# Storing the residual early, adding the feed-forward's output onto it by accumulating DMAs from GpSimd, and taking the last two block products by token tile

## What is computed

```python
x = x + rms_norm(merged @ w_o, norm_mix_post)
hf = rms_norm(x, norm_ff_pre)
ff = jnp.square(jax.nn.relu(hf @ w_ff_in)) @ w_ff_out     # 1024 -> 4096 -> 1024
return x + rms_norm(ff, norm_ff_post)
```

## Time and profile before

| what | us |
|---|---|
| median of 3 runs (785.39 to 787.23) | 785.5 |
| the profiled execution, its own time | 785.12 |
| its span, first to last instruction | 783.4 |
| TensorE busy in it | 765.7 (98%) |
| VectorE busy | 529.3 (68%) |
| ScalarE busy | 365.2 (47%) |
| GpSimd busy | 58.4 (7%) |
| mean granted TensorE clock | 0.996 of full speed |

### The profile page before, as it was taken

The page is one execution under the profiler, slowest core; times in us unless marked ns, Lnnn a source line. Parts: engine busy times, 40 slices in busy tenths (PEclk is TensorE's granted clock), DMA queues, the critical chain, the costliest instruction groups (busy, mean ns, idle before and its releaser), DMA issues.

```text
span 783.4 us, 9921 instructions
## 1 busy us (share of the span) xinstructions
PE 765.7 (98%) x3640; PEld 640.7 (82%) x3640; DVE 529.3 (68%) x883; ACT 365.2 (47%) x609; POOL 58.4 (7%) x110
## 2 busy tenths in 40 slices
PE   7999999999999999999999999999999999999994
PEld 6888888888887888888888998888887888878873
DVE  5624667677777336885635779746895579667897
ACT  4522656666565744232325545544443444334542
POOL 3000000022223003000001200000000000000002
PEclk9999999999999999999999999999999999999998
DMA  8333232212132532326331452136003620262002
GB/s 295 109 114 101 70 92 79 83 55 82 55 83 80 188 101 61 114 75 242 107 108 54 161 186 57 54 139 211 27 3 104 259 65 1 56 240 81 0 1 108
DMA packets 91581, 80.29 MB, mean 102 GB/s; under 512 B 2833, under 2 KB 77585, under 8 KB 91537
## 3 DMA queue, kind: packets, MB, share of 16 engines
q1 hardware_dynamic: 90864, 79.70, 31.5%
q10 hardware_dynamic: 672, 0.01, 0.0%
HBM read 77.60 MB, written 2.10 MB: 102 GB/s over the span
## 4 chain that ended last, share of the span: by engine, by line
PE 90%; DVE 6%; ACT 1%; DMA 1%; issue 0%; SPq 0%; POOL 0%; DVEq 0%; POOLq 0%; ACTq 0%
PE acc L1382 26%; PE acc L1384 26%; PE acc L1383 26%; DVE w_lo L1213 2%; PE aux L1383 1%; PE aux L1384 1%; PE aux L1382 1%; DVE sum L1236 1%; DMA w_raw<-in_w_in 1%; PE aux L1569 1%; PE aux L1495 1%; PE aux L1494 1%; PE aux L1504 1%; PE acc L1523 1%; PE acc L1520 1%; PE aux L1477 1%
## 5 line engine op out<-in xcount | busy, mean ns | idle before, releaser
L1382 PE MATMUL acc<-actB_hi,w_hi 128*128 128x512 f32 (+1 forms) x544 | 207.3, 381 | 0.8 <-DVE sum L1318 0.8
L1384 PE MATMUL acc<-actB_hi,w_lo 128*128 128x512 f32 (+1 forms) x544 | 205.4, 378 | 0.0
L1383 PE MATMUL acc<-actB_lo,w_hi 128*128 128x512 f32 (+1 forms) x544 | 205.2, 377 | 0.0
L931 DVE TENSOR_TENSOR w_lo<-w_raw,w_hi 128x1024 fp32r<-128x1024 f32 x72 | 87.8, 1223 | 83.9 <-ACT w_hi L648 83.1
L1382 PEld LDWEIGHTS acc<-actB_hi,w_hi 128*128 128x128 f32 x544 | 102.5, 188 | 19.6 <-DVE w_lo L1209 1.6
L1384 PEld LDWEIGHTS acc<-actB_hi,w_lo 128*128 128x128 f32 x544 | 102.4, 188 | 18.9
L1383 PEld LDWEIGHTS acc<-actB_lo,w_hi 128*128 128x128 f32 x544 | 102.5, 188 | 18.1
L648 ACT ACTIVATE w_hi<-w_raw 128x1024 fp32r<-128x1024 f32 x72 | 75.4, 1052 | 71.1 <-PE acc L1384 68.8
L1382 PE MATMUL acc<-w_hi,actB_hi 128*128 128x512 f32 x160 | 62.7, 392 | 1.5 <-DVE actB_lo L941 1.3
L1384 PE MATMUL acc<-w_hi,op_lo 128*128 128x512 f32 x160 | 63.5, 397 | 0.0
L1383 PE MATMUL acc<-w_lo,op_hi 128*128 128x512 f32 x160 | 63.4, 396 | 0.0
(11 more groups left out here) (192 smaller groups left out, 1292.1 us busy)
## 6 DMA issues: line engine op xcount, KB each, us to landing
w_raw<-in_w_in SPq DMA_DIRECT2D x44, 512.0 KB, 3.9
w_raw<-in_w_ff_in SPq DMA_DIRECT2D x32, 512.0 KB, 4.0
down_raw<-in_w_ff_out SPq DMA_DIRECT2D x16, 1024.0 KB, 6.9
w_raw<-in_w_b SPq DMA_DIRECT2D x8, 512.0 KB, 3.6
w_raw<-in_w_a SPq DMA_DIRECT2D x8, 512.0 KB, 3.5
w_raw<-in_w_o SPq DMA_DIRECT2D x8, 512.0 KB, 3.8
x<-in_x SPq DMA_DIRECT2D x4, 512.0 KB, 7.5
x<-in_x SPq DMA_DIRECT2D x1, 2048.0 KB, 9.0
```

What stands on the lines that cost most here:

```text
L931: nc.vector.tensor_tensor(w_lo[:, j], w_raw[:, j], w_hi[:, j].bitcast(F32), ALU.subtract).then_inc(lo_made, 1)
L1382: nc.tensor.matmul(o, a_hi, b_hi, start=first, stop=False)
L1383: nc.tensor.matmul(o, a_hi, b_lo, start=False, stop=False)
L1384: return nc.tensor.matmul(o, a_lo, b_hi, start=False, stop=last)
```

## The change

Four things.

1. SyncE stores the four tiles of `x1` to the result in chunk 0 of the feed-forward, behind the loads of that chunk and ahead of the load of `g_ff_post`. They count on a new semaphore, `x1_stored`.
2. The final sums of VectorE go. `scale` multiplies a half in place by `rstd` and the gain in one `scalar_tensor_tensor` (`sum * rstd * g`), and GpSimd issues, for each of the eight halves, a DMA with `accum_op=ALU.add` that adds the 128 x 512 tile onto the result in HBM. GpSimd waits for `x1_stored` before the first and for all eight at the end. The gains into `down_raw` go too. The SBUF reserved for DMAs issued by GpSimd is doubled (`SCRATCH`).
3. TensorE takes the last two products by token tile: P3 and P2 for p = 0, then P3 and P2 for p = 1.
4. VectorE, ScalarE and GpSimd follow that order: the merges for p = 0, then for p = 1, with the scaling of tiles 2 and 3 between them; the adds of tile 2 are written before the `rstd` of tile 0 on GpSimd, those of tile 3 before the `rstd` of tile 1, the other four last.

```diff
-SCRATCH = 1024
+SCRATCH = 2048
...
+LAST_TWO = [(CHUNKS - 1, "P3"), (CHUNKS - 1, "P2")]
...
@@ SyncE @@
                 load_down(c, 3)
                 if c == 0:
+                    for t in range(TT):
+                        sp.wait_ge(x1_made, t + 1)
+                        sp.dma_start(out_v[:, t], x1[:, t]).then_inc(x1_stored, 16)
                     sp.wait_ge(pe_done, UNIT_DONE[U_FF - 1])
                     sp.dma_start(g_ff_post[:], norm_ff_post[0:1, :].to_broadcast([P, D])).then_inc(g_ff_in, 16)
-            for n, t in enumerate((2, 3)):
-                sp.wait_ge(y_made, n + 1)
-                sp.dma_start(out_v[:, t], x1[:, t]).then_inc(stored, 16)
-            for n, (t, h) in enumerate(((0, 1), (0, 0), (1, 1), (1, 0))):
-                cols = slice(h * COL, (h + 1) * COL)
-                sp.wait_ge(y_made, 2 + n + 1)
-                sp.dma_start(out_v[:, t, cols], x1[:, t, cols]).then_inc(stored, 16)
-            sp.wait_ge(stored, 16 * 6)
@@ GpSimd @@
-            for first, n in ((2, 0), (0, 4)):
...
+            def add_out(n, src, t, half):
+
+                pool.wait_ge(y_made, n + 1)
+                nc.gpsimd.dma_start(out_v[:, t, half * COL:(half + 1) * COL], src,
+                                    accum_op=ALU.add).then_inc(stored, 16)
+
+            ff_half(slice(2, 4), 2)
+            ff_rstd(2, 3)
+            ff_rstd(3, 4)
+            pool.wait_ge(x1_stored, 16 * TT)
+            add_out(0, sum6[:, 0], 2, 1)
+            add_out(1, sum4[:, 0], 2, 0)
+            ff_half(slice(0, 1), 5)
+            ff_rstd(0, 6)
+            add_out(2, sum6[:, 1], 3, 1)
+            add_out(3, sum4[:, 1], 3, 0)
+            ff_half(slice(1, 2), 7)
+            ff_rstd(1, 8)
+            for p in range(2):
+                add_out(4 + 2 * p, sum1[:, p], p, 1)
+                add_out(5 + 2 * p, sum2[:, p], p, 0)
+            pool.wait_ge(stored, 16 * 2 * TT)
@@ ScalarE @@
             for p in range(2):
-                ff_square(4 + p, sum1[:, p], 1, p)
-            for p in range(2):
-                ff_square(6 + p, sum2[:, p], 0, p)
+                ff_square(4 + 2 * p, sum1[:, p], 1, p)
+                ff_square(5 + 2 * p, sum2[:, p], 0, p)
@@ VectorE @@
+                def scale(o, half, t):
+
+                    dve.wait_ge(rstd_ff, {2: 1, 3: 2, 0: 3, 1: 4}[t])
+                    nc.vector.scalar_tensor_tensor(o, o, rstd[:, 4, t:t + 1],
+                                                   g_ff_post[:, half * COL:(half + 1) * COL],
+                                                   ALU.mult, ALU.mult).then_inc(y_made, 1)
...
+            dve.wait_ge(g_ff_in, 16)
             for p in range(2):
...
+                bank_done("P3", p)
+                merge(sum1[:, p], aux[:, 2 + p], sum1[:, p], signal=ff_ready)
+                if p:
+                    scale(sum1[:, 0], 1, 0)
+                    scale(sum2[:, 0], 0, 0)
+                else:
+                    scale(sum6[:, 0], 1, 2)
+                    scale(sum4[:, 0], 0, 2)
+                bank_done("P2", p)
+                merge(sum2[:, p], acc[:, p], sum2[:, p], signal=ff_ready)
+                if p == 0:
+                    scale(sum6[:, 1], 1, 3)
+                    scale(sum4[:, 1], 0, 3)
+            scale(sum1[:, 1], 1, 1)
+            scale(sum2[:, 1], 0, 1)
@@ TensorE @@
+            for p in range(2):
+                for c, name in LAST_TWO:
+                    bank_free(c, name, p)
+                    for h in range(2):
+                        if p == 0:
+                            operands(c, name, h)
+                        m = item_product(c, name, h, p)
+                    m.then_inc(pe_done, 1)
```

More of the change, by code:

```diff
@@ L164, in _pe_counts @@
             u = U_FF + product_item(c, name, 0)
-            if (c, name) != (CHUNKS - 1, PRODUCTS[-1]):
-                n += 1
-                unit_done[u] = n
+            if (c, name) in LAST_TWO:
+                continue
+            n += 1
+            unit_done[u] = n
             for p in range(2):
@@ L171, in _pe_counts @@
             unit_done[u + 1] = n
+    for p in range(2):
+        for c, name in LAST_TWO:
+            n += 1
+            bank_done[U_FF + product_item(c, name, 1), p] = n
     return unit_done, bank_done
@@ L628, in _, with ff_rstd, ff_half @@
                     inv_sqrt(ssq[:, 3, t:t + 1], 3, t, rstd_x1)
-            for first, n in ((2, 0), (0, 4)):
-                pair = slice(first, first + 2)
-                pool.wait_ge(ff_squared, n + 2)
-                after(nc.gpsimd.tensor_scalar(ssq_eps[:, 1, pair], ssq[:, 5, pair], EPS, None, ALU.add))
-                for p in range(2):
[L634 to L638, removed]
+            def ff_rstd(t, squared):
+                pool.wait_ge(ff_squared, squared)
+                after(nc.gpsimd.tensor_tensor(var_eps[:, 4, t:t + 1], ssq_eps[:, 1, t:t + 1],
+                                              ssq[:, 4, t:t + 1], ALU.add))
+                power(4, t, rstd_ff)
+            def ff_half(tiles, squared):
+                pool.wait_ge(ff_squared, squared)
+                after(nc.gpsimd.tensor_scalar(ssq_eps[:, 1, tiles], ssq[:, 5, tiles], EPS, None, ALU.add))
+            def add_out(n, src, t, half):
[18 more added lines that the diff above has]
+            pool.wait_ge(stored, 16 * 2 * TT)
         @block.scalar
@@ L1344, in _ @@
                             ins.then_inc(ff_ready, 1)
[L1345 to L1348, removed]
                     lo_ahead(item(c, at + 1))
[L1350 to L1355, removed]
-                            gain(2 + p, sum4[:, p], 0, 2 + p)
@@ L1357, in _ @@
-                    if last and name == "P3":
-                        for p in range(2):
-                            gain(4 + p, sum1[:, p], 1, p)
-                        for t in (2, 3):
-                            dve.wait_ge(rstd_ff, t - 1)
-                            dve.wait_ge(gained, 4)
-                            nc.vector.scalar_tensor_tensor(x1[:, t], down_raw[:, t, 0], rstd[:, 4, t:t + 1], x1[:, t],
-                                                           ALU.mult, ALU.add).then_inc(y_made, 1)
@@ L1365, in _ @@
-            for p in range(2):
-                dve.wait_ge(pe_done, BANK_DONE[UNITS - 1, p])
-                nc.vector.tensor_tensor(sum2[:, p], acc[:, p], sum2[:, p], ALU.add).then_inc(ff_ready, 1)
-                gain(6 + p, sum2[:, p], 0, p)
-                dve.wait_ge(rstd_ff, 3 + p)
-                for h in (1, 0):
-                    cols = slice(h * COL, (h + 1) * COL)
-                    dve.wait_ge(gained, 5 + p if h else 7 + p)
-                    nc.vector.scalar_tensor_tensor(x1[:, p, cols], down_raw[:, p, 0, cols], rstd[:, 4, p:p + 1],
-                                                   x1[:, p, cols], ALU.mult, ALU.add).then_inc(y_made, 1)
+            dve.wait_ge(g_ff_in, 16)
@@ L1660, in _ @@
                 for name in PRODUCTS:
-                    if (c, name) == (CHUNKS - 1, PRODUCTS[-1]):
-                        for p in range(2):
-                            bank_free(c, name, p)
-                            for h in range(2):
-                                if p == 0:
-                                    operands(c, name, h)
-                                m = item_product(c, name, h, p)
-                            m.then_inc(pe_done, 1)
+                    if (c, name) in LAST_TWO:
                         continue
```

9 lines of the change are left out of this document (2 added, 7 removed).

## The result

The changed kernel takes 790.0 us (median of 7 runs, 789.53 to 791.88) against 785.5 us: ratio 1.006, 95% interval 1.0051 to 1.0069. It is slower by 4.5 us, and outside the predicted range. The profiled execution took 790.44 us, its span is 788.7.

What follows compares the result with a forecast made beforehand. The prediction took the 10.0 us tail behind TensorE's last matmul as the bound, 3.8 us of it order. Span end 775.8 + 3.0 + 1.0 + 2.9 + 0.4 = 783.1 against 783.4; forecast 785.2 us, range 782.2 to 788.9.

Steps and rivals of the forecast that it cites:

- The reading of before: Tail behind the last matmul: 3.8 us of its 10.0 us are VectorE taking two token tiles in order, not work.
- TensorE's stall: Second half of P2 for p = 0 waits for its low part: 0 to 0.2 us, taken as 0.
- The early stores: SyncE's four stores of x1 near 463.1 cost nothing; without the cover expected, some 10 us.
- d: Time one accumulating DMA holds GpSimd's queue at issue: taken as 1.0 us.
- rival B: Adds ahead of the inverse roots in GpSimd's queue delay them, from d = 1.4 on; 788.4 us at d = 1.6; chance 0.14.
- w: Time from the end of an add's issue to its landing: 1.67 + 1.2 = 2.87 us.
- R + 3d + d + w: Last four adds at the kernel's end, issued in a row after tile 1's root: 775.8 + 3.0 + 1.0 + 2.9.
- R: Moment the inverse root of tile 1 is ready on GpSimd: 775.8, against 3.7 us later before.
- rival C: Last four adds queue on the DMA engines, 4 x 1.8 = 7.2 us: median 787.6 us; chance 0.13.
- the end: From the last landing to the end of the span: 0.4 us.

Runs made afterwards that it cites:

- e1_ring4096: The changed kernel with SCRATCH 4096 instead of 2048, twice the room for GpSimd's DMAs: 788.58 us, ratio 1.0037 to the kernel before.
- e5_ring1024: The changed kernel with SCRATCH 1024 instead of 2048, half the room for GpSimd's DMAs: 794.62 us, ratio 1.0121 to the kernel before.
- e12_whole_tiles: The changed kernel with SCRATCH 4096 and four whole-tile adds of 512 KB instead of eight of 256 KB: 786.34 us, ratio 1.0012.
- e2_plain4096: The changed kernel with SCRATCH 4096 and GpSimd's eight DMAs as plain stores without accumulation (result lacks the residual): 783.50 us, ratio 0.9968.
- e9_add_tile2: The changed kernel with accumulating adds for tile 2 alone; other tiles keep their residual in SBUF, stored by SyncE: 783.84 us, ratio 0.9980.
- e13_old_pe_add2: The kernel before with VectorE's end reordered, GpSimd adding tile 2 alone, SyncE storing the other six halves: 783.45 us, ratio 0.9974.

## Why the prediction was wrong

- **The reading of before was right.** The tail was an order of VectorE, the root of tile 1 came 3.3 us earlier (776.25 against about 779.5), and the last scaling ended at 777.7 for 777.2. Of the missing 0.45 us TensorE's stall is 0.2 (from 766.25 to 766.90 are two intervals of 0.23 and 0.19 more; I had 0 to 0.2, taken as 0); the rest is a drift of 0.2 us ahead of this stage.
- **The early stores** cost nothing, as said.
- **d was near.** I took 1.0 for an issue on GpSimd. Where nothing is waited for, the adds start 0.5 to 0.8 us apart and their rows are 0.9 to 1.5 us long; the last three before the wait went in 2.7 us. This term was not at fault, and at d below 1.4 rival B didn't arise with the room at 2048.
- **w was near for one add alone:** 3.6 - 0.87 = 2.7 us against 2.87.
- **The step that failed is the path of the last four adds, "R + 3d + d + w": one issued behind the other, each landing as if it were alone.** It took neighbouring adds to overlap on the DMA engines. They hardly do: an add of 256 KB holds the engines for 1.8 to 1.9 us, and in e1_ring4096, where nothing else waits, the time to landing grows from 3.8 to 7.6 us within the last four. That is rival C, whose price of 1.8 us per add was right and whose chance of 0.13 was too small; the sign that the prediction named for it, landing times that grow, is there in the changed kernel too (4.8, 5.8 and 6.6 us). Rival C gave 787.6; e1_ring4096 measured 788.6. On its span the difference is 1.2 us: 0.5 of it at the last landing (785.6 for 785.1), where R alone is 0.45 later than assumed, and 0.7 behind it, as the span ended 1.1 us after the landing and not 0.4. That the first four adds held up the last four is at most 0.3 us: the engines were free of them at 777.9, and the first of the last four, issued at 776.2, would have reached the engines near 777.7, if it took as long to get there as the eighth (issued at 784.26, engines busy from 785.7).
- **A mechanism was missing altogether:** the room that the change doubles. I listed `SCRATCH` as part of the change and gave it no price. Seven accumulations use it up, and the eighth waited 5.3 us. That cost 1.4 us net (790.0 against 788.6 with the room at 4096), since the engines were busy until 783.4 for most of the wait.
- **The sum, term by term:** end of the span forecast 783.1, measured 788.7. R +0.45; three intervals between issues, 3d = 3.0, became 8.0 (5.3 of it is the wait), +5.0; d + w 3.9 became 3.6, -0.3; the end +0.4. Together +5.6.
- **A rule of the Trainium skill:** page "SBUF — State Buffer", section "Who interferes with whom", has it that VectorE's instructions with two inputs in SBUF contend with GpSimd where it reads SBUF and not where it only writes. A root beside the scalings or gains took 0.88 to 1.02 us against 0.57 alone, which agrees. An accumulating issue took 0.86 to 0.90 us with VectorE idle (e5_ring1024, e12_whole_tiles) and 0.94 to 1.08 beside the scalings (e12_whole_tiles, whose issues don't overlap each other). So the issue is stretched as well, by up to 0.2 us. No run shows whether an issue reads SBUF, so this settles nothing against the rule.

What stays open: why an accumulation costs the engines nearly three times a plain store, and the rule by which the room is given back (the last wait of e5_ring1024). That the destination is read first is my reading of the first; nothing here isolates it, and the profile counts 77.60 MB read from HBM in the kernel before and in the changed one alike.

## What to carry to other kernels

An accumulating DMA takes a vector operation away but costs the DMA engines 1.8 to 1.9 us per 256 KB, and several of them queue; put them where the engines are idle and nothing waits, never at the end of the kernel. When two tiles follow each other serially in the chain although the matmuls of both are over, look at the program order of the engine that merges them before touching TensorE's order. And when a change alters the size of a buffer or ring, price what happens when it is full.

## What the runs showed of the hardware

- An accumulating DMA (SBUF to HBM, 128 rows of 2 KB, from GpSimd) alone: issue 0.87 us, landing 3.6 us from its start; a plain one from GpSimd: 0.54 to 0.63 and 2.4 to 2.8 us in e2_plain4096's last group; a plain one from SyncE: 0.33 and 2.0 us, and 2.5 to 2.6 for the last of three issued 0.7 us apart (e9_add_tile2, e13_old_pe_add2). Time of all 16 engines: 1.8 to 1.9 us for an add, 0.65 for a plain store, 2.9 for an add with rows of 4 KB.
- A span that ended on GpSimd's wait for its DMAs ended 0.6 to 1.1 us after the last landing (the changed kernel, e1_ring4096, e2_plain4096, e5_ring1024, e12_whole_tiles), one that ended on SyncE's 0.4 us after it (the kernel before).
- With `SCRATCH` 1024, 2048 and 4096, the first wait came before the fourth add, before the eighth, and not within eight. Plain stores from GpSimd passed without a wait at 2048. The wait shows in the profile as idle time of GpSimd put down to "issue", without a releaser, and ends 0.2 to 0.3 us after the add issued just before has landed.
